# Another order in the mixers of a two-block kernel: one weight rounding, one unit's scores, one unit's transposes

## The chip, the cores and the metric

The kernel runs on one core of a Trainium2 chip. The metric is the device time of one launch in microseconds (us), as the median of several runs. Beside the runs stands one execution recorded by the profiler, from which the rows below are read.

## The reference

The program computes two transformer-like blocks over 256 tokens of 1,024 features in float32. The first has two layers of SwiGLU feed-forwards around a convolution mixer and a differential attention. The second, in which the change lies, is this (cut):

```python
xn = rmsnorm(h, norm1_g[l])
proj = xn @ w_in[l]                       # 5,400 columns
a_q, a_f, a_i, a_g, b_q, b_kv, b_gate, m_gate = jnp.split(proj, SPLIT_POINTS, axis=-1)
y_a = hgrn2_mixer(a_q, a_f, a_i, a_g, lb_all[l], hgrn_norm_g[l])   # recurrence, 4 chunks of 64
y_b = nsa_mixer(b_q, kc, vc, ks_, vs_, kw_, vw_, b_gate, ...)      # sparse attention, 3 branches
g_a, g_b = jnp.split(jax.nn.sigmoid(m_gate), 2, axis=-1)
merged = g_a * (y_a @ w_br_a[l]) + g_b * (y_b @ w_br_b[l])
h = h + merged @ w_out[l]
hn = rmsnorm(h, norm2_g[l])
h = h + jnp.square(jax.nn.relu(hn @ w_ff1[l])) @ w_ff2[l]
```

The sparse attention has a compressed branch (blocks of 32 tokens through a small two-layer network with a gelu, then a softmax over 15 blocks), a selected branch and a window branch. With 256 tokens the last two are causal attentions over all tokens, for 8 heads each.

## The kernel before

**Weights.** Each weight matrix goes through the core in pieces of 128 by 2,048 values, in one fixed order (`plan`). A piece has one of four slots, each with a `raw`, a `whi` and a `wlo` buffer. SyncE (SP) loads `raw`; ScalarE (ACT) rounds it into `whi` (L1535, the high part); VectorE (DVE) subtracts to get `wlo` (L2148, the low part). `split_to(i)` on ACT or DVE does this for all pieces up to number i. TensorE (PE) forms each product from three matmuls, high by high, high by low, low by high (L572 to L574, `mm3`). A slot's `raw` is free once DVE is done, its `whi` and `wlo` once PE is done.

**The groups.** `w_in` comes in eleven groups of columns, at most 512 wide, g = 0 to 10. Each has two pieces, `a` for the first four blocks of the features, `b` for the last four. For groups 6 to 10 PE's products are cut into quarters of 12 matmuls, `win(g, "a0")`, `"a1"`, `"b0"`, `"b1"`, which are laid between the small work of the mixers. ACT and DVE copy a finished group out of PSUM (`group(g)` and `evac(g)`, L1860, L1905 and L2542, L2594).

**The order.** Each engine has its own list of work, written out by hand in `pe_mixers`, `act_mixers` and `dve_mixers`, and runs it strictly in that order. They meet through semaphores. POOL has almost nothing to do here.

**The recurrence.** After group 2, PE transposes the columns C_Q and then C_F of `proj` into the two PSUM banks TB 0 and TB 1 (`bank_transposes`, L609). ACT copies the first out as `hq` (L1875) and the second with a sigmoid as `hf` (L1878). PE may write a bank only when it has been read out (`t_used`). DVE scales `hf`, ACT takes the logarithm (L1880), DVE runs a scan over it, and so on.

**The sparse attention.** It has eight units u = 0 to 7, each a pair of heads of one branch:

- `scores(u)` on PE (L1201, L1205) writes half of the PSUM tensor DD, once `exps(u - 2)` has read that half.
- `maxima(u)` on DVE (L2674), `exps(u)` on ACT (L1935), `normalise(u)` on DVE (L2682 to L2687).
- `probs_t(u, c)` on PE (L609), c = 0 and 1, transposes the probabilities into bank TB c; `probs(u, c)` on ACT (L1944) copies them to `at`.
- `values(u)` on PE (L1221, L1223) multiplies with the values into bank u % 2, and `outputs(u)` on DVE (L2696 or L2699) takes the result out.

**The compressed branch.** `compress(i, half)` on PE (L1235) is the first layer, for keys (i = 0) and values (i = 1); `parts_copy(i)` on ACT (L1950) copies it out. `hidden_sums(i)` on PE (L1244) adds up its parts into bank i, `gelu_keys` and `gelu_values` on ACT (L1954, L1960) take the gelu. Then come `keys_of_blocks` on PE (L1253) with `kc_block_copy` on ACT (L1969), `values_of_blocks` (L1262) with `block_values_diag` on DVE (L2704), `block_scores` (L1272), and a softmax on DVE and ACT.

**Turns of the banks.** TB 0 and TB 1 are used in turn by all of this. The lists MIX0 and MIX1 name the turns of each bank in PE's order; `spot` turns a name into the number that a semaphore must reach. On ACT, behind `gelu_values`, the list goes on unchanged with this:

```python
                split_to(win_at(10) + 1)
                probs(4, 0)
                exps(5)
                split_to(win_at(10) + 1 + 1)
                kc_block_copy()
                split_to(seg["branch"] + 0 + 1)
                probs(4, 1)
                evac(9)
                exps(6)
```

Of the kernel before, what the change touches and what calls it, by code (L numbers as in the profile page):

```python
# [191 lines left out]
def two_blocks(nc, a, out, stop=None):  # L192
    ctx = ExitStack()
    with ctx:
# [7 lines left out]
        ent, seg = st.entries, st.segment  # L202
# [229 lines left out]
            return P3(C_F, 512)[:, j // 2, (j % 2) * S + lo_:(j % 2) * S + lo_ + n_]  # L432

        MIX0 = ["tq0", "tk0", "tk2", "T00", "T10", "V0", "T20", "V2", "T30", "gtk", "T40", "W2", "V4", "T50", "T60", "T70", "pcT", "V6", "fa0", "fm0", "fm2"]
        MIX1 = ["tq1", "tk1", "tk3", "T01", "T11", "V1", "T21", "T31", "gtv", "V3", "T41", "VC", "T51", "T61", "V5", "T71", "V7", "fa1", "fm1", "fm3"]

        def spot(base, name):

# [7 lines left out]
        def win_bank(g):  # L446

            return DD if g == 10 else GU
# [117 lines left out]
        def _(pe):  # L566
# [533 lines left out]
            def pe_mixers():  # L1100
# [31 lines left out]
                def win(g, part):  # L1132

                    e0, e1 = ent[win_at(g)], ent[win_at(g) + 1]
                    e, m = (e0 if part[0] == "a" else e1), e0.cols
                    if part[1] == "0":
                        pe.wait_ge(lo_done[e.slot], e.raw_before + 1)
                    wh, wl = view(whi[e.slot], e), view(wlo[e.slot], e)
                    half = int(part[1])
                    seq = [(k, t) for k in (2 * half, 2 * half + 1) for t in range(TT)] if part[0] == "a" else \  # L1140
                          [(k, half) for k in range(4)]
                    for k, t in seq:
                        kk, ts = k + (0 if part[0] == "a" else 4), slice(t * P, (t + 1) * P)
                        mm = mm3(win_bank(g)[:, t, 0:m], xh[:, kk, ts], xl[:, kk, ts], wh[:, k, :], wl[:, k, :],
                                 start=(kk == 0), stop=(kk == 7))
                    if part == "b0":
                        mm.then_inc(gu_ready, 1)
                        n.gu += 1
                    if part in ("a1", "b1"):
                        mm.then_inc(used[e.slot], 1)  # L1150
# [41 lines left out]
                def scores(u):  # L1192

                    _, j, g, kk, _ = unit(u)
                    if u >= 2:
                        pe.wait_ge(exp_done, u - 1)
                    pair = DD[:, 2 * (u % 2):2 * (u % 2) + 2, :]
                    for half in range(2):
                        for c in range(2):
                            pick, rows = causal(half, c)  # L1200
                            pe.matmul(diagonal(pair[:, c, :]), pick, rows, start=(half == 0), stop=False, skip_group_check=True)  # L1201
                    for c in range(2):
                        cs = slice(64 * c, 64 * c + 64)
                        for qi in range(TT):
                            mm = pe.matmul(pair[:, c, keys(qi)], qT2(j, qi * P, P)[cs, :], kk[cs, g, 0:(qi + 1) * P],  # L1205
                                           start=False, stop=True, skip_group_check=True)
                    mm.then_inc(sc_ready, 1)

                def probs_t(u, c):

                    pe.wait_ge(norm_ready, u + 1)
                    bank_transposes(c, [(q * P, sm[:, u % 2, c, q * P:(q + 1) * P]) for q in range(3)])

                def values(u):

                    b, vals = u % 2, unit(u)[4]
                    for c in range(2):
                        pe.wait_ge(t_used[c], spot(base, f"T{u}{c}"))
                    pe.wait_ge(t_used[b], n.t[b])
                    for c in range(2):  # L1220
                        pe.matmul(TB[64 * c:64 * c + 64, b, 0:S], vals[:, 0, :], at[:, b, 3 * P * c:3 * P * c + S], start=True, stop=False)  # L1221
                    for c in range(2):
                        mm = pe.matmul(TB[64 * c:64 * c + 64, b, P:S], vals[:, 1, :], at[:, b, 3 * P * c + S:3 * P * (c + 1)],  # L1223
                                       start=False, stop=True)
                    mm.then_inc(t_ready[b], 1)
                    n.t[b] += 1
# [12 lines left out]
                def hidden_sums(i):  # L1239

                    pe.wait_ge(parts_ready, i + 1)
                    pe.wait_ge(t_used[i], n.t[i])
                    for hh in range(2):
                        mm = pe.matmul(TB[:, i, 32 * hh:32 * hh + 30], parts[:, i, hh * P:(hh + 1) * P], quads[:, 0:2 * NCMP],  # L1244
                                       start=True, stop=True)
                    mm.then_inc(t_ready[i], 1)
                    n.t[i] += 1
# [94 lines left out]
                win(8, "b0")  # L1342
                probs_t(1, 0)
                probs_t(1, 1)
                values(0)
                win(8, "b1")
                values(1)
                scores(3)
                probs_t(2, 0)
                probs_t(2, 1)  # L1350
                for t in range(TT):
# [5 lines left out]
                values(2)  # L1357
                compress(1, 0)
                compress(1, 1)
                probs_t(3, 0)  # L1360
                probs_t(3, 1)
                hidden_sums(0)
                scores(5)
                pe.wait_ge(parts_ready, 2)
                win(9, "a0")
                hidden_sums(1)
                values(3)
                probs_t(4, 0)
                win(9, "a1")
                scores(6)  # L1370
                pe.wait_ge(t_used[0], spot(base, "gtk"))
                keys_of_blocks()
                probs_t(4, 1)
                win(9, "b0")
                win(9, "b1")
                values(4)
                pe.wait_ge(t_used[1], spot(base, "gtv"))
# [147 lines left out]
        def _(act):  # L1525
# [11 lines left out]
            def split_to(i):  # L1537
                while n.next < min(i, len(ent)):
                    split(ent[n.next])
                    n.next += 1  # L1540
# [305 lines left out]
            def act_mixers():  # L1846
                def group(g):

                    if g in (1, 3):
                        n.d += 1  # L1850
                        act.wait_ge(d_ready, n.d)
                        src, read = DD[:, 0, :], d_used[0]
                    else:
                        n.gu += 1
                        act.wait_ge(gu_ready, n.gu)
                        src, read = GU[:, 0, :], gu_used[0]
                    if g == 0:
                        act.wait_ge(rs_ready, order("pre7"))
                    m = ent[seg["w_in"] + 2 * g].cols
                    nc.scalar.activation(P3(512 * g, m)[:, 0, :], src[:, 0:m], ACT.Copy, scale=rcol("pre7", 0)).then_inc(read, 1)  # L1860
                    if g < 9:
                        split_to(seg["w_in"] + 2 * (g + 2) + 2)

                act.wait_ge(lbt_ready, 1)
                nc.scalar.activation(lbe, lbt, ACT.Exp).then_inc(lbe_ready, 1)
# [7 lines left out]
                for b in range(2):  # L1873
                    bank(b)
                    nc.scalar.activation(hq[:, b * 512:(b + 1) * 512], TB[:, b, :], ACT.Copy).then_inc(t_used[b], 1)  # L1875
                for b in range(2):
                    bank(b)
                    nc.scalar.activation(hf[:, b * 512:(b + 1) * 512], TB[:, b, :], ACT.Sigmoid).then_inc(t_used[b], 1)  # L1878
# [50 lines left out]
                def exps(u):  # L1929

                    b = u % 2
                    act.wait_ge(mx_ready, u + 1)
                    for c in range(2):
                        for qi in range(TT):
                            e = nc.scalar.activation(sm[:, b, c, keys(qi)], DD[:, 2 * b + c, keys(qi)], ACT.Exp,  # L1935
                                                     bias=nmx[:, b, c, qi:qi + 1], accum_out=den8[:, u, c, qi:qi + 1])
                    e.then_inc(exp_done, 1)

                def probs(u, c):

                    if u >= 2:
                        act.wait_ge(t_ready[u % 2], spot(base, f"V{u - 2}"))
                    act.wait_ge(t_ready[c], spot(base, f"T{u}{c}"))
                    nc.scalar.activation(at[:, u % 2, 3 * P * c:3 * P * (c + 1)], TB[:, c, 0:3 * P], ACT.Copy).then_inc(t_used[c], 1)  # L1944

                def parts_copy(i):

                    e = ent[seg["cmp"] + 2 * i + 1]
                    act.wait_ge(lo_done[e.slot], e.raw_before + 1)
                    nc.scalar.activation(parts[:, i, :], GU[:, i, 0:S], ACT.Copy).then_inc(parts_ready, 1)  # L1950
# [71 lines left out]
                probs(2, 1)  # L2022
                exps(3)
                parts_copy(0)
                probs(3, 0)
                probs(3, 1)
                parts_copy(1)
                exps(4)
                gelu_keys()
                gelu_values()  # L2030
                split_to(win_at(10) + 1)
# [1036 lines left out]
```

## Time and profile before

| | |
|---|---|
| median of 3 runs | 1386.77 us (1386.51 to 1387.38) |
| the profiled execution | 1386.2 us, its span 1384.5 us |
| PE busy | 1360.1 us, 98% of the span |
| DVE busy | 814.5 us, 59% |
| ACT busy | 680.2 us, 49% |
| POOL busy | 43.8 us, 3% |
| DMA | 247.09 MB, mean 178 GB/s |

The span runs from the first to the last instruction of the profiled execution; the time of the launch has a little more around it. Busy time counts the instructions of an engine without its waits. For PE the time of a matmul is modelled, and matmuls overlap in the rows: one may show 0.39 us while the next starts 0.23 us later. The distance between the starts is then what one costs. The mixers lie at about 987 to 1180 us.

### The profile page before, as it was taken

How to read it: one execution, taken by the hardware profiler on the slowest of the kernel's cores; microseconds unless marked ns; L12 is line 12 of the kernel's file. 1: busy time of each engine (PE TensorE's matmuls, PEld its weight loads, DVE VectorE, ACT ScalarE, POOL GpSimd, SP SyncE). 2: the span in 40 equal slices, each digit the busy share in tenths (PEclk: the TensorE clock that was granted, in tenths of full speed). 3: DMA queues.
4: the chain of work that ended last, by engine and by line, in shares of the span. 5: the costliest groups of instructions: out<-in, count | busy, mean ns of one | idle time of the engine just before them, and what ended most of it. 6: DMA issues, size and time to landing. Idle time of an engine off the chain costs nothing.

```text
span 1384.5 us, 17405 instructions
## 1 busy us (share of the span) xinstructions
PE 1360.1 (98%) x6525; PEld 1116.3 (81%) x6525; DVE 814.5 (59%) x898; ACT 680.2 (49%) x873; POOL 43.8 (3%) x112
## 2 busy tenths in 40 slices
PE   8999999999999999999999999999999999999997
PEld 6888888888888888888887788888878778888886
DVE  5545567665555655544568754555767668654553
ACT  5444454454444554444467654444664466544442
POOL 3000000000000000000000100000000000000000
PEclk9999999999999999999999999999999999999999
DMA  8655656445556554555743255656454354565540
GB/s 291 211 193 192 216 173 216 157 160 193 182 182 226 183 182 147 188 182 184 243 165 107 91 184 189 194 191 229 167 182 152 106 172 138 190 220 188 178 165 31
DMA packets 160236, 247.09 MB, mean 178 GB/s; under 512 B 9086, under 2 KB 104504, under 8 KB 160184
## 3 DMA queue, kind: packets, MB, share of 16 engines
q1 hardware_dynamic: 160072, 246.33, 54.0%
q8 instruction: 35, 0.57, 0.2%
q14 instruction: 17, 0.14, 0.0%
q10 hardware_dynamic: 112, 0.05, 0.0%
HBM read 245.30 MB, written 1.05 MB: 178 GB/s over the span
## 4 chain that ended last, share of the span: by engine, by line
PE 96%; ACT 2%; DVE 1%; issue 0%; POOL 0%; DMA 0%; POOLq 0%; ACTq 0%; DVEq 0%
PE GU L572 15%; PE GU L574 15%; PE GU L573 15%; PE DD L572 12%; PE DD L574 12%; PE DD L573 12%; PE GU L637 4%; PE TB L609 3%; PE TB L765 2%; PE GU L644 2%; ACT xh L1547 1%; PE DD L1205 0%; PE GU L1470 0%; PE TB L1221 0%; PE GU L1473 0%
## 5 line engine op out<-in xcount | busy, mean ns | idle before, releaser
L2148 DVE TENSOR_TENSOR wlo<-raw,whi 128x2048 fp32r<-128x2048 f32 x224 | 509.3, 2282 | 268.6 <-ACT whi L1535 268.4
L1535 ACT ACTIVATE whi<-raw 128x2048 fp32r<-128x2048 f32 x223 | 424.1, 1908 | 175.7 <-PE DD L574 168.1
L572 PE MATMUL GU<-whi,xh 128*128 128x512 f32 x928 | 367.4, 396 | 0.6 <-DVE hid L2265 0.5
L574 PE MATMUL GU<-whi,xl 128*128 128x512 f32 x928 | 362.1, 390 | 0.0
L573 PE MATMUL GU<-wlo,xh 128*128 128x512 f32 x928 | 361.1, 389 | 0.0
L574 PEld LDWEIGHTS GU<-whi,xl 128*128 128x128 f32 x928 | 174.2, 188 | 37.4
L572 PEld LDWEIGHTS GU<-whi,xh 128*128 128x128 f32 x928 | 174.3, 188 | 36.3 <-issue 2.0
L573 PEld LDWEIGHTS GU<-wlo,xh 128*128 128x128 f32 x928 | 174.5, 188 | 34.4
L572 PE MATMUL DD<-whi,hth 128*128 128x512 f32 x496 | 194.8, 393 | 0.0
L574 PE MATMUL DD<-whi,htl 128*128 128x512 f32 x496 | 193.2, 389 | 0.0
L573 PE MATMUL DD<-wlo,hth 128*128 128x512 f32 x496 | 193.0, 389 | 0.0
L1635 ACT ACTIVATE hth<-TB 128x512 fp32r<-128x512 f32 x54 | 31.6, 599 | 165.8 <-PE TB L765 165.8
L574 PEld LDWEIGHTS DD<-whi,htl 128*128 128x128 f32 x496 | 93.1, 188 | 19.5
L573 PEld LDWEIGHTS DD<-wlo,hth 128*128 128x128 f32 x496 | 93.2, 188 | 18.8
L572 PEld LDWEIGHTS DD<-whi,hth 128*128 128x128 f32 x496 | 93.1, 188 | 18.7
L1646 ACT ACTIVATE sg<-GU,rs 128x256 f32<-128x256 f32 x88 | 41.9, 476 | 113.1 <-PE GU L574 106.8
L572 PE MATMUL DD<-whi,xh 128*128 128x512 f32 (+1 forms) x240 | 93.8, 391 | 0.2 <-DVE xl L2455 0.2
L574 PE MATMUL DD<-whi,xl 128*128 128x512 f32 (+1 forms) x240 | 92.0, 384 | 0.0
L573 PE MATMUL DD<-wlo,xh 128*128 128x512 f32 (+1 forms) x240 | 91.9, 383 | 0.0
L2258 DVE TENSOR_TENSOR htl<-TB,hth 128x512 fp32r<-128x512 f32 x54 | 36.6, 690 | 90.1 <-ACT hth L1635 90.1
L2265 DVE SCALAR_TENSOR_TENSOR hid<-GU,rs,sg 128x256 f32<-128x256 f32 x88 | 42.2, 481 | 43.4 <-ACT sg L1646 43.4
L572 PEld LDWEIGHTS DD<-whi,xh 128*128 128x128 f32 x240 | 45.1, 188 | 9.1 <-DVE xl L2455 0.6
(300 smaller groups left out, 1071.2 us busy)
## 6 DMA issues: line engine op xcount, KB each, us to landing
raw<-in_w_ffn_down SPq DMA_DIRECT2D x88, 512.0 KB, 4.4
raw<-in_w_ffn_gate SPq DMA_DIRECT2D x86, 512.0 KB, 4.0
raw<-in_w_ffn_up SPq DMA_DIRECT2D x86, 512.0 KB, 5.0
raw<-in_w_ff SPq DMA_DIRECT2D x64, 512.0 KB, 4.4
raw<-in_w_in SPq DMA_DIRECT2D x40, 512.0 KB, 4.6
raw<-in_w_conv_in SPq DMA_DIRECT2D x24, 512.0 KB, 4.9
raw<-in_w_kv SPq DMA_DIRECT2D x16, 512.0 KB, 4.7
raw<-in_w_conv_out SPq DMA_DIRECT2D x8, 512.0 KB, 4.6
```

Of the source, the lines that this page charges most:

```text
L572: pe.matmul(dst, h, w_h, start=start, stop=False)
L573: pe.matmul(dst, h, w_l, start=False, stop=False)
L574: return pe.matmul(dst, l, w_h, start=False, stop=stop)
L609: mm = pe.transpose(TB[0:m, bank, c:c + r], src, ident[0:r, 0:r])
L637: pe.matmul(dst[:, 0:m], xh[:, 4 * half + k, ts], view(w[e.slot], e)[:, k, :], start=(half == 0 and k == 0 and w is whi), stop=False)
L644: mm = pe.matmul(dst[:, 0:m], xl[:, 4 * half + k, ts], view(whi[e.slot], e)[:, k, :], start=False, stop=(half == 1 and k == 3))
L1535: nc.scalar.activation(whi[s][:, 0:size], raw[s][:, 0:size], ACT.Copy).then_inc(hi_done[s], 1)
L1635: nc.scalar.activation(hth[:, 2 * b:2 * b + 2, :].rearrange("p k n -> p (k n)"), TB[:, b, :], ACT.Copy).then_inc(hth_done[b], 1)
L1646: nc.scalar.activation(sg[:, t, 0:FG], GU[:, t, 0:FG], ACT.Silu, scale=rcol(pre, t)).then_inc(sg_done[t], 1)
L2148: nc.vector.tensor_tensor(wlo[s][:, 0:size], raw[s][:, 0:size], whi[s][:, 0:size].bitcast(F32), ALU.subtract).then_inc(lo_done[s], 1)
L2258: nc.vector.tensor_tensor(htl[:, 2 * b:2 * b + 2, :].rearrange("p k n -> p (k n)"), TB[:, b, :], hth[:, 2 * b:2 * b + 2, :].rearrange("p k ...
L2265: nc.vector.scalar_tensor_tensor(out=hid[:, t, 0:FG], in0=GU[:, t, FG:512], scalar=rcol(pre, t), in1=sg[:, t, 0:FG], op0=ALU.mult, op1=ALU ...
```

## The change

It moves work within the lists of PE and ACT; nothing is added or taken away, and the lists of DVE and SP are as they were.

- ACT rounds the second piece of group 4 behind the two copies of `hq`, and not ahead of them in `group(2)`.
- PE computes `scores(3)` two places up, ahead of `values(0)`.
- PE runs `scores(5)` and the first quarter of group 9 ahead of `probs_t(3, 0)` and `probs_t(3, 1)`, `scores(6)` ahead of `hidden_sums(0)`, then `values(3)`, the second quarter of group 9, and only then `hidden_sums(1)`. The third quarter moves ahead of `keys_of_blocks`.
- In bank 1's list of turns, V3 and gtv (the turn of `hidden_sums(1)`) change places.
- ACT runs `exps(4)` and `parts_copy(1)` ahead of `probs(3, 0)` and `probs(3, 1)`.

```diff
-        MIX1 = [..., "T31", "gtv", "V3", "T41", ...]
+        MIX1 = [..., "T31", "V3", "gtv", "T41", ...]
...
                 probs_t(1, 1)
+                scores(3)
                 values(0)
                 win(8, "b1")
                 values(1)
-                scores(3)
                 probs_t(2, 0)
...
                 values(2)
                 compress(1, 0)
                 compress(1, 1)
-                probs_t(3, 0)
-                probs_t(3, 1)
-                hidden_sums(0)
                 scores(5)
                 pe.wait_ge(parts_ready, 2)
                 win(9, "a0")
+                probs_t(3, 0)
+                probs_t(3, 1)
+                scores(6)
+                hidden_sums(0)
+                values(3)
+                win(9, "a1")
                 hidden_sums(1)
-                values(3)
                 probs_t(4, 0)
-                win(9, "a1")
-                scores(6)
+                win(9, "b0")
                 pe.wait_ge(t_used[0], spot(base, "gtk"))
                 keys_of_blocks()
                 probs_t(4, 1)
-                win(9, "b0")
                 win(9, "b1")
                 values(4)
...
-                        split_to(seg["w_in"] + 2 * (g + 2) + 2)
+                        split_to(seg["w_in"] + 2 * (g + 2) + (1 if g == 2 else 2))
...
                     nc.scalar.activation(hq[:, b * 512:(b + 1) * 512], TB[:, b, :], ACT.Copy).then_inc(t_used[b], 1)
+                split_to(seg["w_in"] + 2 * 4 + 2)
...
                 exps(3)
                 parts_copy(0)
+                exps(4)
+                parts_copy(1)
                 probs(3, 0)
                 probs(3, 1)
-                parts_copy(1)
-                exps(4)
                 gelu_keys()
                 gelu_values()
```

## Rows read from the trace of the kernel before

**Rows 1.** The page: granted TensorE clock in 40 slices, in tenths.

```profile
PEclk9999999999999999999999999999999999999999
```

**Rows 2.** PE's waits, 950 to 1160 us: who, for whom, total, times, longest.

```profile
PE TB L609 <- ACT hid L1875: 1.7, 1, 1.7
PE TB L1221 <- ACT junk L1960: 0.6, 1, 0.6
...
PE TB L1244 <- ACT at L1944: 0.4, 1, 0.4
PE TB L1221 <- ACT at L1944: 0.3, 1, 0.3
PE TB L609 <- DVE hid L2696: 0.3, 1, 0.3
```

**Rows 3.** Order of time around group 2: start, duration, what, [idle before, releaser].

```profile
1010.64 1.91 ACT L1535 ACTIVATE whi<-raw 128x2048 fp32r<-128x2048 f32 x1 [0.29 <-PE GU L574]
...
1012.46 1.07 ACT L1875 ACTIVATE hid<-TB 128x512 f32<-128x512 f32 x2
1013.09 1.14 PE L609 MATMUL TB<-ident,proj 128*128 128x128 f32 x8 [1.67 <-ACT hid L1875]
...
1022.48 0.69 ACT L1860 ACTIVATE proj<-DD,rs 128x512 f32<-128x512 f32 x1 [3.97 <-PE DD L574]
```

**Rows 4.** Order of time on PE, 1101 to 1134 us.

```profile
1101.65 0.51 PE L1201 MATMUL DD<-hth 64*128 64x256 f32 x4
...
1115.58 0.52 PE L1244 MATMUL TB<-quads,proj 128*128 128x30 f32 x4
...
1116.72 0.65 PE L1221 MATMUL TB<-at,proj 128*64 128x256 f32 x4 [0.61 <-ACT junk L1960]
...
1117.52 0.55 PE L609 MATMUL TB<-ident,sm 128*128 128x128 f32 x3
1117.83 0.47 PE L572 MATMUL GU<-whi,xh 128*128 128x512 f32 x1
...
1120.76 0.51 PE L1201 MATMUL DD<-hth 64*128 64x256 f32 x4
...
1121.96 0.29 PE L1253 MATMUL TB<-small,junk 128*128 128x30 f32 x1
...
1128.37 0.65 PE L1221 MATMUL TB<-at,proj 128*64 128x256 f32 x4
...
1130.93 0.88 PE L609 MATMUL TB<-ident,sm 128*128 128x128 f32 x6
...
1133.45 0.77 PE L609 MATMUL TB<-ident,sm 128*128 128x128 f32 x5
```

**Rows 5.** Order of time on ACT, 1116 to 1147 us.

```profile
1116.14 0.43 ACT L1960 ACTIVATE junk<-TB 128x120 f32<-128x120 f32 x2 [1.49 <-PE TB L1244]
...
1118.16 0.49 ACT L1944 ACTIVATE at<-TB 128x384 f32<-128x384 f32 x1 [0.57 <-PE TB L609]
...
1124.99 0.49 ACT L1944 ACTIVATE at<-TB 128x384 f32<-128x384 f32 x1
...
1146.10 1.90 ACT L1535 ACTIVATE whi<-raw 128x2048 fp32r<-128x2048 f32 x1
```

**Rows 6.** Order of time on DVE, 1101 to 1134 us.

```profile
1101.77 0.42 DVE L2696 COPY hid<-TB 128x256 f32<-128x256 f32 x1
...
1122.75 1.33 DVE L2148 TENSOR_TENSOR wlo<-raw,whi 128x1120 fp32r<-128x1120 f32 x1 [2.54 <-ACT whi L1535]
...
1128.48 0.75 DVE L2594 TENSOR_SCALAR proj<-GU,rs 128x512 f32<-128x512 f32 x1
1129.29 0.42 DVE L2699 TENSOR_TENSOR hid<-hid,TB 128x256 f32<-128x256 f32 x1
...
1131.03 1.02 DVE L2674 TENSOR_REDUCE small<-DD 128x2 f32<-128x256 f32 x2 [0.50 <-PE DD L1205]
1131.97 0.17 DVE L2682 RECIPROCAL small<-small 128x4 f32<-128x4 f32 x1
```

More of the change, by code:

```diff
@@ L434, in two_blocks @@
         MIX0 = ["tq0", "tk0", "tk2", "T00", "T10", "V0", "T20", "V2", "T30", "gtk", "T40", "W2", "V4", "T50", "T60", "T70", "pcT", "V6", "fa0", "fm0", "fm2"]
-        MIX1 = ["tq1", "tk1", "tk3", "T01", "T11", "V1", "T21", "T31", "gtv", "V3", "T41", "VC", "T51", "T61", "V5", "T71", "V7", "fa1", "fm1", "fm3"]
+        MIX1 = ["tq1", "tk1", "tk3", "T01", "T11", "V1", "T21", "T31", "V3", "gtv", "T41", "VC", "T51", "T61", "V5", "T71", "V7", "fa1", "fm1", "fm3"]
         def spot(base, name):
```

## Prediction, made before the change was run

> **What bounds the kernel now.** I read the page first. TensorE (PE) works through nearly the whole span, and its clock line is at the top tenth in all 40 slices [rows 1]. A new order of the same work can therefore win only PE's idle time, and lose only by making more of it. The second view is PE's own list of waits over the mixers, 950 to 1160 us [rows 2]. It holds five that this diff touches: 1.7 us on the copies of hq, and 0.3, 0.3, 0.4 and 0.6 us in the sparse attention, 3.3 us in all. That sum, 0.24% of the time, is the most that this change can give. The third view is the order of time of each engine around the edits: PE and ScalarE (ACT) around group 2 [rows 3], then PE [rows 4], ACT [rows 5] and VectorE (DVE) [rows 6] from 1095 to 1150 us. There the reader is to see how far behind PE the other two engines work when PE comes to need them: that distance is what the second edit spends.
>
> **Edit A, one weight rounding behind the copies.** PE transposes C_Q from 1010.38. ACT first rounds the second half of group 4 (1010.64, 1.91 us), then copies hq at 1012.46; PE, 0.63 us behind that, goes on at 1013.09 after 1.67 us of idle time [rows 3]. With the rounding moved behind both copies, ACT is free at about 1010.4 and waits for the first bank's transposes. From the start of a bank of transposes to the copy that reads it takes 0.64 us (1117.52 on PE, 1118.16 on ACT) [rows 4, 5]: hq starts at 1011.0 and not 1012.46. **Gain 1.45 us**, with some 0.2 us of idle time left. Bounds: 1.1 if the copy sees PE later, 1.67 as the whole wait. The rounding then runs at 1012.1 to 1014.0; before, ACT was through with the copies at 1012.46 + 1.07 = 1013.5, so the sigmoid is some 0.4 late. The logarithm and the scan on DVE follow it, also 0.4 late, while ACT's next piece that waits for PE moves forward from 1022.48, ahead of which ACT stood idle for 3.97 us [rows 3]. So 0.4 and 1.45 fit into 3.97: cost nothing, and without that cover 0.4. DVE's low part of that half ends 0.6 us later, and so SP's refill of its raw buffer starts later, for a rounding two groups away. POOL has no part in it. From here to 1097 PE has no wait [rows 2], and what others do is released by it, so the 1.45 us travel on. I leave them out of the following times, which are those of the trace before, and add them at the end.
>
> **Edit B, PE's order.** scores(3) ahead of values(0) needs only exps(1), long done; its 1.2 us cover the 0.34 that values(0) waited. But probs_t(2,1) now comes right behind values(1), and its bank is freed by DVE's outputs(1). In the old order that ran at 1101.77 for 0.42 while PE had scores(3) to do [rows 4, 6]; with 0.14 us from a release to PE (the first of the two hq copies, 1.07 us together, ends at about 1012.95, and PE goes on at 1013.09 [rows 3]) it is free at 1102.33, and PE, at 1101.65 plus 0.4 for probs_t(2,0), waits **0.28**. So this swap gives 0.06. The 0.29 and 0.40 at unit 3's transposes and hidden_sums(0) go: outputs(2) and probs(3,0) get a quarter of group 9, 2.9 us, or scores(6), 1.2 us, of cover. parts_copy(1) now stands behind exps(4), but exps(4) no longer waits for the probs of unit 3, so it ends about 0.5 us before PE asks for it; if that cover is gone it costs tenths.
>
> **What stands behind hidden_sums(1).** It now comes behind values(3), win(9,a1) and scores(6). In the old order values(3) took 1117.52 - 1116.72 = 0.80 us, win(9,a1) 1120.76 - 1117.83 = 2.93 and scores(6) 1121.96 - 1120.76 = 1.20, in all 4.93 us [rows 4]. Its start moves from 1115.58 to 1115.58 + 4.93 - 0.34 - 0.29 - 0.40 + 0.28 = 1119.76. ACT's list is unchanged here: gelu_values waits for exactly this, and behind it are queued two roundings of 1,120 columns, probs(4,0), a table load, exps(5), kc_block_copy, a rounding of 2,048 columns and probs(4,1). In the trace this takes from 1116.14 to 1124.99 + 0.49 = 1125.48, 9.34 us, with only 0.57 idle ahead of probs(4,0) [rows 5], and that idle time goes: 8.77. New: 1119.76 + 0.56 + 8.77 = 1129.09, and PE can take values(4) at 1129.23. PE itself, with 0.34 + 0.29 + 0.40 + 0.61 won and 0.28 lost, arrives at 1128.37 - 1.36 = 1127.01. It **waits 2.2 us**, and is at values(4) 0.86 later than before instead of 1.36 earlier.
>
> DVE is next. Its low part of the second 1,120-column piece (1122.75) lies 6.04 us of work behind gelu_values: 1120.32 + 6.04 = 1126.36, 3.61 later. From 1122.75 to group 9's evacuation at 1128.48 DVE had no idle time, so that moves to 1132.09, outputs(4) (1129.29) to 1132.8, and the bank of probs_t(5,0) is free at 1132.8 + 0.42 + 0.14 = 1133.36. PE arrives at 1129.23 + (1130.93 - 1128.37) = 1131.79 and **waits 1.6**; it is now 2.43 behind the old time. The same queue has block_values_diag, maxima(7) (0.94) and normalise(6) to go, 2.68 us from outputs(4) to normalise(6) less 0.50 of idle time and less 0.25 of small gaps that close: normalise(6) at 1134.7, seen by PE 1.48 later (1131.97 to 1133.45 before), 1136.2. probs_t(6,0) moves from 1133.45 to 1136.2: **B costs 2.75** [rows 4, 6]. Bounds: 0.86, if DVE's part is absorbed, to 3.3, if the last two waits add up.
>
> After that the three engines move together. The branch weights' raw buffers are freed 3 to 3.6 us later and SP refills them later, but the rounding of the third one is at 1146.10 [rows 5], over 20 us behind. I cost it at nothing.
>
> **Sum.** +2.75 - 1.45 = +1.3 us. On the profiled execution (span 1384.5, time 1386.2) that is 1387.5; the median of the runs is 1386.77, so 0.6 above it, and I add the sum to the median: **1388.1**. Its own range is 1387.0 to 1389.4.
>
> **Rivals.** (1) The ACT queue doesn't reach PE: gelu_values isn't held, or the queue behind it is under 6.7 us of work. Then only waits go: -1.45 - 1.64 + 0.28 = -2.8, **1384.0**. For it: ACT is half idle on the page. Against: the 8.77 us are dense in the trace. (2) The wait at values(4) comes, but DVE catches up: 0.86 - 1.45 = -0.6, **1386.2**. Against: DVE shows no gap in 1122.75 to 1128.48. (3) Edit A gives nothing, because the sigmoid's chain, 0.4 late, holds PE: from 3.97 us of lost cover on; then +2.75 alone, **1389.5**. (4) The new waits bring PE's clock down: it decides if one of them is long enough. The granted clock stayed at the top through the 1.67 us wait [rows 1, 2]; the new one of 2.2 is longer. At the lower of its two levels a quarter of group 9 (1117.83 to 1120.76) would take 2.9 more, **1391.0**.
>
> The Trainium skill, "TensorE: Matmul & The Clock Gate", Part 1, says that the array falls back to half rate when it has stood idle, and asks for no long idle gaps between bursts. By that rule this change, which swaps five short waits for two longer ones, is the wrong way round; the trace neither shows nor excludes it at 2.2 us, and the sum doesn't use it.
>
> **How the numbers follow.** A measurement of this kernel tells some 0.2%, 2.8 us, from no change: faster means under 1384.0, slower over 1389.5. Forecast 0.58, rival 1 0.12, rival 2 0.16, rival 3 0.11, rival 4 0.03. Half of rival 1 and the low tail of rival 2 make faster 0.08. Half of rival 3, rival 4 and the upper tail of the forecast make slower 0.15. The rest, 0.77, is no change. The range leaves out most of rival 1 and rival 4: 1385.0 to 1390.0.
>
> **What the new profile would show.** A: PE's 1.67 falls to about 0.2, and hq starts 0.64 after C_Q's transposes. B: no wait of values(0), values(3) or hidden_sums(0); one of 0.3 for outputs(1) at probs_t(2,1); gelu_values behind an idle stretch of some 4 us; one of about 2.2 at values(4) for probs(4,1); one of about 1.6 at probs_t(5,0) for outputs(4). PE's idle time from 1095 to 1145 grows by some 2.7. The prediction is wrong if values(4) doesn't wait, or if both waits appear and a later stretch gives the time back.

## The result, and the profile after

The changed kernel takes 1390.77 us (median of 20 runs, 1387.92 to 1391.80) against 1386.47 (20 runs, 1385.45 to 1387.68): a ratio of 1.0029, 95% interval 1.0022 to 1.0036. It is slower by 4.3 us. Forecast were 1.3 us, and the time lies 0.8 above the top of the range. The profiled execution took 1390.74 us, with a span of 1389.0.

The page's clock line shows what the forecast's sum doesn't have. It is no longer the same in all 40 slices [rows 1]:

```profile
PEclk9999999999999999999999999999999989999999
```

PE's waits from 950 to 1160 us, the view of [rows 2], have become few. Of the 3.3 us that the edit aimed at, 0.2 are left; one new wait stands first:

```profile
PE TB L1221 <- ACT at L1945: 2.2, 1, 2.2
PE GU L637 <- ACT xh L1547: 0.4, 1, 0.4
PE TB L609 <- ACT hid L1875: 0.2, 1, 0.2
```

Around group 2, in order of time (start, duration, what, idle time before), the view of [rows 3]. In this execution everything runs 0.39 us earlier than in the one before, up to this place: C_Q's transposes start at 1009.99, where the prediction had 1010.38.

```profile
1009.99 1.03 PE L609 MATMUL TB<-ident,proj 128*128 128x128 f32 x8
...
1010.63 1.09 ACT L1875 ACTIVATE hid<-TB 128x512 f32<-128x512 f32 x2 [0.67 <-PE TB L609]
...
1011.28 1.15 PE L609 MATMUL TB<-ident,proj 128*128 128x128 f32 x8 [0.25 <-ACT hid L1875]
1011.60 1.92 ACT L1535 ACTIVATE whi<-raw 128x2048 fp32r<-128x2048 f32 x1
```

hq starts 0.64 us after the transposes and PE waits 0.25 in place of 1.67: edit A gives 1.42. Then PE from 1113 to 1148 us, the view of [rows 4]:

```profile
1117.68 0.52 PE L1244 MATMUL TB<-quads,proj 128*128 128x30 f32 x4
...
1124.38 0.39 PE L574 MATMUL GU<-whi,xl 128*128 128x512 f32 x1
1126.96 0.70 PE L1221 MATMUL TB<-at,proj 128*64 128x256 f32 x4 [2.19 <-ACT at L1945]
...
1129.61 1.65 PE L1205 MATMUL DD<-gain,proj 64*128 64x128 f32 x8
1131.19 1.54 PE L609 MATMUL TB<-ident,sm 128*128 128x128 f32 x6
1132.52 3.46 PE L1272 MATMUL GU<-small,proj 128*128 128x30 f32 x16
1135.80 1.52 PE L609 MATMUL TB<-ident,sm 128*128 128x128 f32 x6
...
1147.54 1.22 PE L609 MATMUL TB<-ident,proj 128*128 128x128 f32 x8
```

PE waits 2.19 us at values(4), right behind two quarters of group 9. Behind the wait the same instructions are slow: the six transposes of probs_t(5) take 1.54 us and not 0.88 [rows 4]. The same stretch by windows (length, busy time of PE, weight load, DVE, ACT and POOL, then the granted clock, DMA share, GB/s) says why:

```profile
1125.00:1127.60 2.60, 0.64 (x6) 0.58 (x8) 2.53 (x7) 2.42 (x3) 0.00 (x0) 0.97 0.52 147
1127.60:1142.00 14.40, 14.40 (x75) 12.49 (x73) 11.24 (x26) 5.61 (x22) 0.00 (x0) 0.53 0.38 130
1142.00:1147.50 5.50, 5.36 (x41) 4.17 (x39) 1.11 (x2) 3.15 (x4) 0.00 (x0) 1.00 0.00 0
```

For about 14 us the granted clock is at or near its lower level, 1.2 GHz (mean 0.53). PE counts as busy throughout, so the page's 98% hides it; its busy time grew by 5.1 us (1365.2) with the same 6,525 matmuls.

ACT, the view of [rows 5], and DVE, that of [rows 6]:

```profile
1118.24 0.43 ACT L1961 ACTIVATE junk<-TB 128x120 f32<-128x120 f32 x2 [3.73 <-PE TB L1244]
...
1126.37 0.49 ACT L1945 ACTIVATE at<-TB 128x384 f32<-128x384 f32 x1
```

```profile
1124.17 1.32 DVE L2149 TENSOR_TENSOR wlo<-raw,whi 128x1120 fp32r<-128x1120 f32 x1 [3.12 <-ACT whi L1535]
...
1129.89 0.75 DVE L2595 TENSOR_SCALAR proj<-GU,rs 128x512 f32<-128x512 f32 x1
1130.55 0.41 DVE L2700 TENSOR_TENSOR hid<-hid,TB 128x256 f32<-128x256 f32 x1
```

From gelu_values to the end of probs(4,1) is 8.62 us, 1118.24 to 1126.86 (forecast 8.77). outputs(4) ends at 1130.96, and PE starts probs_t(5,0) at 1131.19: the second forecast wait is not in PE's list, because PE, at the low clock, comes late itself. The runs agree with their clocks: the two fastest of the 20, 1387.92 and 1388.41 us, have a mean clock of 0.996 over the span, the five at 0.993 take 1390.74 to 1391.80. The profiled execution is one of these five, so its 14 us are the long case and not the usual one.

### The profile page after: what moved, and what is told of

Its sections match the earlier page's. It is cut to its first block, busy times and chain, and to the rows that moved or that the text cites. A ratio compares the mean times of both kernels' runs of the same rounds, so it can differ in the third digit from the quotient of the medians.

```text
span 1389.0 us, 17405 instructions
## 1 busy us (share of the span) xinstructions
PE 1365.2 (98%) x6525; PEld 1121.3 (81%) x6525; DVE 814.4 (59%) x898; ACT 680.3 (49%) x873; POOL 43.0 (3%) x112
## 3 DMA queue, kind: packets, MB, share of 16 engines
HBM read 245.30 MB, written 1.05 MB: 177 GB/s over the span
## 4 chain that ended last, share of the span: by engine, by line
PE 95%; ACT 2%; DVE 1%; issue 0%; POOL 0%; DMA 0%; POOLq 0%; ACTq 0%; DVEq 0%
PE GU L572 15%; PE GU L574 15%; PE GU L573 15%; PE DD L572 12%; PE DD L574 12%; PE DD L573 12%; PE GU L637 4%; PE TB L609 3%; PE TB L765 2%; PE GU L644 2%; ACT xh L1547 1%; PE DD L1205 0%; PE TB L1221 0%; ACT whi L1535 0%; PE GU L1470 0%
```

## The experiments

Two theories were put against each other. **Clock**: the wait at values(4) brings PE's clock down, and that costs some 3 of the 4.3 us. **Queue**: the late lists of ACT and DVE cost all of it, and the clock is low only while PE would have waited anyway. The kernel before ran beside each group of experiments: 1386.29 (24 runs) beside e1, e3, e4 and e5, 1386.47 (20) beside e2, e6 and e9, 1386.37 (15) beside e7. Its mean clock was 0.998 or 0.999 in all 59 runs. A mean clock is taken over the whole span; where in the span the clock was low is known only for the one profiled execution of each kernel.

**e1_rounding_only.** Edit A on the kernel before.

```diff
-                        split_to(seg["w_in"] + 2 * (g + 2) + 2)
+                        split_to(seg["w_in"] + 2 * (g + 2) + (1 if g == 2 else 2))
...
                     nc.scalar.activation(hq[...], TB[:, b, :], ACT.Copy).then_inc(t_used[b], 1)
+                split_to(seg["w_in"] + 2 * 4 + 2)
```

> The kernel before with edit A alone: the second rounding of group 4 behind the copies of hq. Both theories: PE's wait for hq falls from 1.67 us to 0.25, no other wait appears, the clock stays 1.00. 1.4 us less than before, 1385.1 us.

1384.73 us (11 runs, 1384.32 to 1385.69), ratio 0.9991 (0.9983 to 1.0000): 1.56 less than before. In its profile PE's wait for hq is 0.2, and the other four of [rows 2] stand as they were. A gives what was forecast, and no later wait takes it back. By the times alone this is at the edge of the noise; the trace, where the wait shrinks from 1.67 to 0.25 us, settles it.

**e4_order_only.** The changed kernel without edit A.

```diff
-                        split_to(seg["w_in"] + 2 * (g + 2) + (1 if g == 2 else 2))
+                        split_to(seg["w_in"] + 2 * (g + 2) + 2)
...
-                split_to(seg["w_in"] + 2 * 4 + 2)
```

> The changed kernel without edit A, so PE's order alone. Both theories: the wait at values(4) is 2.2 us again, the clock falls behind it, and the time is 1.4 us over that of the changed kernel, 1392.2. If the gain of A is lost in the changed kernel, it is 1390.8.

1390.69 us (6 runs, 1389.53 to 1394.46), ratio 1.0039 (1.0027 to 1.0051). Both waits of the prediction are in the open here, in PE's list:

```profile
PE TB L1221 <- ACT at L1944: 2.2, 1, 2.2
PE TB L609 <- ACT hid L1875: 1.7, 1, 1.7
PE TB L609 <- DVE hid L2699: 1.5, 1, 1.5
```

Three windows of the same execution:

```profile
1128.00:1131.00 3.00, 2.63 (x24) 1.93 (x24) 3.00 (x4) 2.37 (x10) 0.00 (x0) 1.00 0.94 332
1131.00:1134.00 3.00, 1.60 (x12) 1.42 (x13) 2.95 (x8) 0.96 (x3) 0.00 (x0) 0.94 0.57 169
1134.00:1137.00 3.00, 3.00 (x16) 3.00 (x16) 1.57 (x4) 1.64 (x9) 0.00 (x0) 0.50 0.49 186
```

In this execution the wait of 2.19 us at values(4) leaves the clock at the top, and it falls only behind the second wait, at 1133.6. The expected 1392.2 was missed by 1.5: the six runs differ by up to 4.9 us, four of 1389.53 to 1390.70 with a mean clock of 0.997, and 1393.23 and 1394.46 with 0.994 and 0.993. That A's gain shows in e1 and not in the step from this kernel to the changed one may be due to that; six runs don't settle it.

**e3_wait_filled.** PE does idle transposes where it would wait at values(4). They add work that the reference doesn't have and leave the rest as it is.

```diff
                 win(9, "b1")
+                pe.wait_ge(exp_done, 6)
+                for _ in range(20):
+                    pe.transpose(DD[:, 2, 0:P], ident[:, :], ident[:, :])
                 values(4)
```

> The changed kernel with 20 idle-filling 128x128 transposes (about 2 us, into a PSUM half that nobody uses then) ahead of values(4), where PE waits 2.2 us. Clock theory (the wait at values(4) brings PE's clock down, and the low clock costs some 3 of the 4.3 us): clock 1.00 throughout, waits for outputs(4) and normalise(6) come into the open, time 1387.4. Queue theory (the late lists of ScalarE and VectorE cost the 4.3 us, the low clock lies inside time that PE would have waited anyway): 1390.8, as the changed kernel.

Median 1389.90 (6 runs), ratio 1.0029 (1.0018 to 1.0041). It is a mixture: one run of 1386.98 with a mean clock of 0.998, five of 1389.75 to 1390.69 with 0.996. The profile is that of the first. There the clock is at the top in every window from 1090 to 1155 us, and the DVE wait stands as forecast:

```profile
1125.03 2.35 PE L1378 MATMUL DD<-ident 128*128 128x128 f32 x20
1127.38 0.65 PE L1221 MATMUL TB<-at,proj 128*64 128x256 f32 x4
...
1131.53 1.12 PE L609 MATMUL TB<-ident,sm 128*128 128x128 f32 x6 [1.51 <-DVE hid L2703]
```

So the expectation held in one run. In the other five, of which there is no profile, the mean clock was low, with only the wait of 1.5 us for outputs(4) left to bring it down. The next kernel fills that one too.

**e6_both_filled.**

```diff
+                pe.wait_ge(exp_done, 6)
+                for _ in range(18):
+                    pe.transpose(DD[:, 2, 0:P], ident[:, :], ident[:, :])
                 values(4)
...
                 scores(7)
+                pe.wait_ge(gu_used[0], n.gu)
+                for _ in range(12):
+                    pe.transpose(GU[:, 0, 3 * P:4 * P], ident[:, :], ident[:, :])
                 probs_t(5, 0)
```

> The changed kernel with both waits filled: 18 idle transposes (2.1 us) ahead of values(4), 12 (1.4 us) ahead of probs_t(5,0), into PSUM halves that nobody uses then. They do nothing for the result. Clock theory: no run has a lowered clock, and the time is that of the one run of e3_wait_filled whose clock stayed up, 1387.0, in every run. Queue theory: 1390 or more.

1387.52 us (11 runs, 1386.38 to 1387.79), ratio 1.0006 (0.9997 to 1.0015); the mean clock is 0.998 or 0.999 in every run, as in the kernel before. The order of time on PE, with both waits gone and six transposes back at 0.87 us:

```profile
1125.79 2.13 PE L1378 MATMUL DD<-ident 128*128 128x128 f32 x18
1128.15 0.65 PE L1221 MATMUL TB<-at,proj 128*64 128x256 f32 x4 [0.23 <-issue]
...
1130.71 1.53 PE L1385 MATMUL GU<-ident 128*128 128x128 f32 x12
1132.28 1.12 PE L609 MATMUL TB<-ident,sm 128*128 128x128 f32 x6
...
1135.07 0.87 PE L609 MATMUL TB<-ident,sm 128*128 128x128 f32 x6
```

The windows of the same stretch have the clock at the top:

```profile
1128.00:1131.00 3.00, 2.85 (x27) 2.23 (x28) 3.00 (x4) 2.35 (x10) 0.00 (x0) 1.00 0.93 329
1131.00:1134.00 3.00, 2.87 (x26) 2.45 (x24) 2.93 (x9) 0.99 (x3) 0.00 (x0) 1.00 0.56 186
```

Thirty added transposes make the changed kernel 3.25 us faster. ACT and DVE are as late as in the changed kernel: outputs(4) starts 41.26 us behind probs_t(0,0) in both (1131.73 and 1090.47 here, 1130.55 and 1089.29 there). This decides for the clock theory: 1390.77 - 1387.52 = 3.25 us for the clock, and the intervals of the two ratios don't touch. What is left, 1387.52 - 1386.47 = 1.05, goes to the queues less the gain of A (forecast 1.3); by the interval it isn't clear of zero.

**e7_second_filled.** Only the second filling of e6.

> The changed kernel with only the second wait filled: 12 idle transposes (1.4 us at the high clock) ahead of probs_t(5,0). The wait of 2.2 us at values(4) stays. If that wait alone brings the clock down in nearly every run, most runs come out near 1390.8 plus up to 2 for the transposes at the low clock. If it takes both waits together, most runs keep the clock and come out at 1387.5, as with both filled.

1388.86 us (11 runs, 1388.17 to 1389.83), ratio 1.0018 (1.0009 to 1.0027), mean clock 0.996 or 0.997 in all 11. Against e6 only the first filling is missing, so the wait of 2.2 us is enough by itself to lower the mean clock in each of these runs. The clock comes back sooner than in the changed kernel, so the time is lower than expected:

```profile
1127.61 0.65 PE L1221 MATMUL TB<-at,proj 128*64 128x256 f32 x4 [2.19 <-ACT at L1948]
```

```profile
1128.00:1131.00 3.00, 3.00 (x24) 2.17 (x19) 3.00 (x3) 1.80 (x9) 0.00 (x0) 0.67 0.81 307
1131.00:1134.00 3.00, 3.00 (x23) 2.90 (x22) 2.93 (x9) 0.30 (x1) 0.00 (x0) 0.76 0.71 250
1134.00:1137.00 3.00, 3.00 (x28) 3.00 (x28) 1.72 (x5) 2.97 (x12) 0.00 (x0) 1.00 0.26 100
```

**e2_sums_before_values.** hidden_sums(1) goes ahead of values(3), with its turn; this was to break the one long wait into shorter ones.

```diff
-        MIX1 = [..., "T31", "V3", "gtv", "T41", ...]
+        MIX1 = [..., "T31", "gtv", "V3", "T41", ...]
...
                 hidden_sums(0)
+                hidden_sums(1)
                 values(3)
                 win(9, "a1")
-                hidden_sums(1)
```

> The changed kernel with hidden_sums(1) ahead of values(3), but win(9,a1) ahead of probs_t(4,0) as in it. PE waits 0.6 us at values(3), 1.0 at values(4), 1.6 for outputs(4): shorter waits with about the same sum. Clock theory: if the clock stays up, 1387.0; if 1.0 and 1.6 close together are enough to bring it down, as 1.5 alone was in five of six runs of e3_wait_filled, 1390. Queue theory: 1390 with a high clock.

Median 1389.77 (9 runs, 1386.55 to 1390.86), ratio 1.0022 (1.0013 to 1.0032). Waits of 0.6, 1.3 and 1.5 us; seven runs at 1389.3 to 1390.9 with a mean clock of 0.996 or 0.997, two at 1386.55 and 1387.98 with 0.998. Shorter waits close together do nearly the same. gelu_values runs 3.05 us earlier than in the changed kernel here (1115.19 against 1118.24), and still little is won on ACT: its next copy, probs(4,0), now waits for PE's probs_t(4,0), which stands behind win(9,a1).

```profile
1120.01 0.49 ACT L1945 ACTIVATE at<-TB 128x384 f32<-128x384 f32 x1 [3.37 <-PE TB L609]
```

**e9_probs41_early.** ACT takes probs(4,1) ahead of a rounding.

```diff
-                split_to(seg["branch"] + 0 + 1)
                 probs(4, 1)
+                split_to(seg["branch"] + 0 + 1)
```

> The changed kernel with ScalarE's probs(4,1) ahead of the rounding of the first branch matrix: its queue before values(4) is 1.9 us shorter. PE's wait at values(4) falls to 0.3, but VectorE is as late as before, so the wait for outputs(4) grows to 3.4 us. Clock theory: the clock falls behind that wait, 1390 to 1391. If only ScalarE's queue were the cause, the time would fall by 1.9, to 1388.9, and the clock stay up.

1390.47 us (6 runs, 1390.21 to 1390.95), ratio 1.0032 (1.0019 to 1.0044). PE's list:

```profile
PE TB L609 <- DVE hid L2700: 3.5, 1, 3.5
...
PE TB L1221 <- ACT at L1945: 0.3, 1, 0.3
```

The wait moves from values(4) to probs_t(5,0), to a tenth as worked out from the trace before. To shorten ACT's queue alone gives nothing, since DVE has the same lateness.

**e5_sums_together.** Both sums together, and unit 4's first transposes, probs_t(4,0), ahead of values(3) and the two quarters.

```diff
-        MIX1 = [..., "T31", "V3", "gtv", "T41", ...]
+        MIX1 = [..., "T31", "gtv", "V3", "T41", ...]
...
                 hidden_sums(0)
+                hidden_sums(1)
+                probs_t(4, 0)
                 values(3)
                 win(9, "a1")
-                hidden_sums(1)
-                probs_t(4, 0)
                 win(9, "b0")
```

> The changed kernel with hidden_sums(1) right behind hidden_sums(0), then probs_t(4,0), values(3) and both middle quarters of group 9, and the turns gtv and V3 as before. If what stands behind hidden_sums(1) on ScalarE is what makes PE wait, the wait at values(4) is gone, as is the one for outputs(4), the clock stays 1.00, and the time is 2.1 under before, 1384.4. If the delay comes from another part of the order (scores(3), exps(4) ahead of the probs of unit 3), it stays over 1387.

1384.38 us (11 runs, 1382.95 to 1384.79), ratio 0.9985 (0.9976 to 0.9994), 1.9 us under before, with the rest of the change as it was. This version is faster than both kernels. Its waits in the view of [rows 2]:

```profile
PE GU L637 <- ACT xh L1547: 0.4, 1, 0.4
PE TB L609 <- ACT hid L1875: 0.3, 1, 0.3
PE TB L609 <- DVE hid L2700: 0.2, 1, 0.2
```

So the loss comes from the place of hidden_sums(1) together with that of probs_t(4,0): ACT's roundings, exponentials and probs stand behind both. With both early a loss of 4.3 us becomes a gain of 1.9; hidden_sums(1) early by itself (e2) leaves a loss of 3.3.

## Why the prediction was wrong

**Edit A** was right: 1.45 forecast, 1.42 in the trace, 1.56 in e1. That the delayed sigmoid costs nothing held too.

**scores(3)** was right. The two halves of probs_t(2) take 1.14 us up to compress where six transposes take 0.81, so the 0.28 us wait for outputs(1) is there, too short for the list.

**The wait at values(4)** was right in place, cause and size: 2.2 forecast, 2.19 measured, here and in e4 and e7. Both its ends lie 0.4 us earlier than forecast: values(4) starts 0.44 later than before and not 0.86 (37.67 us behind probs_t(0,0), which starts at 1089.29; before 37.23, from 1091.14). No run says which of the small terms holds the 0.4.

**The wait for outputs(4)** was forecast as 1.6; it is 1.5 in e3 and e4. In the changed kernel it lies under PE's own slowness.

**The sum of the queues**, B at 2.75, is about right: with the clock up (e6) the whole change costs 1.05 us, and with A's 1.56 that is 2.6. Alone it would have given 1387.5, inside the range.

**What failed is the price of the clock.** The sum has no term for it; it stands only as rival 4 under "Rivals", with a chance of 0.03 under "How the numbers follow". It is what happens, in all 20 runs of the changed kernel (mean clock 0.993 to 0.996, against 0.998 to 0.999 in the 59 runs of the kernel before beside the experiments), and e6 puts it at 3.25 us, three quarters of the 4.3. The rival's cause was right, and its price of 2.9 us, taken as one quarter of group 9 at half speed, is near the 3.25 by luck: the slowed work is different (values(4), scores(7), probs_t(5), block_scores, probs_t(6), a quarter of group 10 with its 280 columns), lasts 14 us in the profiled execution, and part of it covers the wait for outputs(4).

The step that led to 0.03 is the sentence that the clock stayed at the top through a wait of 1.67 us, read as if the length of a wait were all that counts. It isn't: 1.5 us, shorter than 1.67, were enough in five runs of e3 out of six. The Trainium skill's rule ("TensorE: Matmul & The Clock Gate", Part 1) was quoted and left out of the sum; the trace of the changed kernel agrees with its direction, with a mean clock of 0.53 over 14.40 us behind 2.19 us of idle time.

**Left open.** Why a wait lowers the clock at one place and not at the other isn't settled here. Both the wait of 1.67 us and that at values(4) stand behind matmuls with 512 columns, the first with eight transposes between. They differ in what comes next: 1.14 us of transposes and then 512 columns again in the one case, values, scores, transposes and block_scores in the other, 5.7 us of them even at the high clock (1128.37 to 1134.09 before). That these small matmuls count is a guess: no run put a wait of the same length into both surroundings. The place isn't all either. After the same wait of 2.19 us the clock falls within 1.5 us of its end in the profiled executions of the changed kernel (1127.4) and of e7 (1129.0), and not in that of e4; it stays low for 13.6, 3.4 and, behind e4's second wait, 6.8 us; and one kernel's runs differ in their mean clock (e4's from 0.997 to 0.993, and by 4.9 us in time). Something that changes from one execution to the next takes part, and nothing here shows what.

## What to carry to other kernels

On an engine that is 98% busy a new order can take away idle time, but first list what is queued on the other engines behind each piece of work that you delay; here 8.6 us of ACT's list hung on one tiny product. One wait of 2 us can cost more than five short ones that add up to more: price it also with the clock at its lower level for the work behind it. The test is cheap: fill the wait with idle matmuls into a free PSUM bank. If the kernel gets faster and the mean granted clock goes up, it was the clock.

## What was not expected of the hardware

- With a PE wait of 2.19 us the mean granted clock was lowered in all 20 runs of the changed kernel and all 11 of e7. In the profiled execution of the changed kernel it was low for 14 us (mean 0.53 over 1127.60 to 1142.00) while PE counted as busy without a gap. In that of e4 it was still 1.00 over 1128 to 1131, behind the same wait.
- Thirty idle transposes, 3.7 us of added PE work, save 3.25 us. Twelve of them in the second wait alone, behind the fall, save 1.9; in the profiled execution of e7 the clock is back at about 1132.4, and in the changed kernel's at about 1141.0.
- A wait of 3.5 us (e9, 1390.47) costs no more than one of 2.2 with the same lateness behind it (1390.77).
